# When the router's weights and the second norm's weight row are loaded, and when the output mixing waits for them

## The chip, the cores and the metric

The kernel runs on one core of one Trainium2 chip. The metric is the device time in microseconds (us) of one execution. The time of the kernel before is the median of three runs.

## The reference, cut to what matters

One layer of a hybrid model on 640 tokens (128 context, 512 latent), width D = 1024. The lines below follow the two scans; the change concerns `norm2_g` and the four `router_*` arrays.

```python
out = jnp.concatenate([o_r, o_g], -1) @ lp['w_out']          # o_r: RWKV-7 group, o_g: gated delta group
x = x + g1 * mix
h = rms_norm(x, lp['norm2_g']) * (1.0 + sc2) + sh2
grp_p = softmax(h @ router_group_w + router_group_b)          # 4 groups, top 1
e_logits = h @ router_expert_w + router_expert_b              # 32 experts, top 2 within the group
x = x + g2 * hier_moe(h, lp)                                  # gated MLP of the chosen experts
```

Inside the RWKV-7 group, before the concatenation, the scan's sum over both directions is normalised per head (lnx_g, lnx_b), a bonus term is added, and the result is multiplied by a gate, `sigmoid(gl) @ rwkv_g2`. The gated delta group is normalised (gdn_norm_g) and multiplied by silu(z).

## The kernel before, in words

The program is one list of instructions for each engine, ordered by hand; engines meet through semaphores. The stages are: the adaLN rows and the input projection, the gated delta scan, the RWKV scan (20 iterations, software pipelined in "slots"), the tail (output mixing, second norm, router, one token tile of 128 after another, five tiles), the sorting of tokens by expert, the experts in blocks, and the final norm. The change is at the seam between the RWKV scan and the tail.

SyncE (SP) issues nearly all loads, in program order. During the scan it stores `new_rwkv` from the tile `hTf` (columns 1536 to 2559, used as `znat`) and waits for the store (`rstate_out`, L473). It then waits for the last preparation step of the scan (L475 and L476) and issues the four constants of the mixing: `g2w`, `lnx_g`, `lnx_b`, `gng` (L477 to L480). Then it waits for the scan's last instruction (L481 and L482) and issues, in this order: `w_out` into `ring` (L483), `x` again (L484 context, L485 latent tokens), the two router weights (L486, L487), the two router biases (L488, L489), and `norm2_g` spread over all partitions into `bias_row` (L490). The last of these, and the five before it that are not `w_out` or `x`, count on the semaphore `cst_in`, nine loads in all.

TensorE (PE), after its last slot, waits for all nine (`pe.wait_ge(cst_in, 16 * 9)`, L973) and then does `mix_pe(0)`: four transposes of the scan's output (L983, "yT") and, when VectorE has subtracted the mean ("yc"), the gate's matmul (L986). It waits for `wout_in` (L1014) and goes through the tiles with `tail_pe(t)`: transposes of the mixed row tile (L993), `mix_pe(t + 1)`, the 16 products with `w_out` (L1001, 32 matmul records of the trace), transposes of the normed tile (L1006), and the router's products (L1010).

VectorE (DVE) waits for the nine constants and for `x` (L1934, L1935), makes the second norm's gain `modk[:, c, 2, :] = (1 + modk) * bias_row` for both conditionings (L1938, two instructions), and starts `mix_dve(0)`: from the reduction at L1957 to the product at L1981 ("o"), the whole of the mixing on one tile. `tail_dve(t)` does `mix_dve(t + 1)` first, then the residual (L1996, L1998), the norm (L2005, L2006) and the router's arithmetic (L2009 and on). Only `tail_dve` reads `x`, `modk[:, c, 2, :]` and the router's values; `mix_dve` reads none of them.

ScalarE (ACT) follows with squares, roots and copies out of PSUM (L1526 to L1549). It waits for none of these loads itself.

Of the kernel before, what the change touches and what calls it, by code (L numbers as in the profile page):

```python
# [10 lines left out]
ALU = mybir.AluOpType  # L11
# [3 lines left out]
P = 128  # L15
# [23 lines left out]
NE, GROUPS, PER_GROUP = 32, 4, 8  # L39
# [86 lines left out]
def program(nc, A, O, book, dbg=None):  # L126
    ctx = ExitStack()
    with ctx:
        sb = lambda name, shape, dt=F32: ctx.enter_context(nc.sbuf_tensor(name, shape, dt))
        sem = lambda name: ctx.enter_context(nc.semaphore(name))  # L130
# [4 lines left out]
        modk = sb("modk", [P, 2, 4, D])  # L135
# [6 lines left out]
        bias_row = sb("bias_row", [P, D])  # L142
# [20 lines left out]
        hTf = hT[:, :, :].rearrange("p k n -> p (k n)")  # L163
# [12 lines left out]
        work = fm[:, FM_V2:FM_V2 + 4, :].rearrange("p a b -> p (a b)")  # L176
# [30 lines left out]
        cst = fm[:, FM_Q2:FM_Q2 + 4, :].rearrange("p a b -> p (a b)")  # L207
        g2w, lnx_g, lnx_b, gng = cst[:, 0:512], cst[:, 512:1024], cst[:, 1024:1536], cst[:, 1536:1664]
        t_st, t_sgl, rtb = cst[:, 1664:1728], cst[:, 1728:1856], cst[:, 1856:1892]
        rw_ = work[:, 0:288].rearrange("p (k n) -> p k n", n=GROUPS + NE)  # L210
# [36 lines left out]
        ident_in, x_again = sem("ident_in"), sem("x_again")  # L247
# [13 lines left out]
        s_mix, s_tail, s_route, s_fin = ST("mix", True), ST("tail", True), ST("route", False), ST("fin", False)  # L261
        s_moe = ST("moe", True)
        wout_in, cst_in, h2_out, tz_out, tok_out, tok_in = (sem(n) for n in ("wout_in", "cst_in", "h2_out", "tz_out", "tok_out", "tok_in"))
# [141 lines left out]
        def _(sp):  # L405
# [67 lines left out]
            sp.wait_ge(rstate_out, 16)  # L473

# [7 lines left out]
            sp.wait_ge(*s_rwkv.pe.at(f"yz{R_ITS - 1}"))  # L482
            sp.dma_start(wout, A["w_out"][0].rearrange("(k p) n -> p k n", p=P)).then_inc(wout_in, 16)  # L483
            sp.dma_start(x[:, 0, :], A["x_prompt"][0]).then_inc(x_again, 16)  # L484
            sp.dma_start(x[:, 1:, :], A["x_sample"][0].rearrange("(t p) d -> p t d", p=P)).then_inc(x_again, 16)  # L485
            sp.dma_start(rw_[:, :, 0:GROUPS], A["router_group_w"][0].rearrange("(k p) n -> p k n", p=P)).then_inc(cst_in, 16)  # L486
            sp.dma_start(rw_[:, :, GROUPS:], A["router_expert_w"][0].rearrange("(k p) n -> p k n", p=P)).then_inc(cst_in, 16)  # L487
            sp.dma_start(rtb[:, 0:GROUPS], A["router_group_b"][0].partition_broadcast(P)).then_inc(cst_in, 16)  # L488
            sp.dma_start(rtb[:, GROUPS:], A["router_expert_b"][0].partition_broadcast(P)).then_inc(cst_in, 16)  # L489
            sp.dma_start(bias_row[:, :], A["norm2_g"][0].partition_broadcast(P)).then_inc(cst_in, 16)  # L490
# [39 lines left out]
        def _(pe):  # L530
# [442 lines left out]
            pe.wait_ge(cst_in, 16 * 9)  # L973
# [40 lines left out]
            pe.wait_ge(wout_in, 16)  # L1014
            tail_pe(0, True)
# [567 lines left out]
        def _(dve):  # L1583
# [350 lines left out]
            dve.wait_ge(cst_in, 16 * 9)  # L1934
            dve.wait_ge(x_again, 32)  # L1935
            dve.wait_ge(*s_route.act.at("silz"))
            for c in range(2):
                nc.vector.scalar_tensor_tensor(modk[:, c, 2, :], modk[:, c, 2, :], 1.0, bias_row[:, :], ALU.add, ALU.mult).then_inc(*s_route.dve.tick("gain2"))  # L1938
            dve.wait_ge(*s_route.dve.so_far())
# [100 lines left out]
            mix_dve(0)  # L2040
            tail_dve(0, 0)
# [56 lines left out]
            for t in range(NT):  # L2098
                c = min(t, 1)
# [36 lines left out]
```

## Time and profile before

| quantity | us |
|---|---|
| median of 3 runs | 2186.66 |
| lowest and highest of them | 2185.87, 2190.09 |
| profiled execution, its own time | 2192.51 |
| its span in the trace | 2190.6 |
| PE busy | 1660.5 (76% of the span) |
| DVE busy | 767.6 (35%) |
| ACT busy | 542.9 (25%) |

The span is what the trace covers; the execution's own time lies 1.91 us above it. Busy time over the span does not say what bounds a given stage. The page also cuts the span into 40 equal slices of 54.8 us and gives the busy share of each in tenths: in the 22nd, 1150 to 1205 us, which holds the end of the scan, it shows 4 tenths for PE, 2 for DVE and 3 for the DMA engines, and in the slice behind it 5, 6 and 0. The finer rows are in the section of rows below.

### The profile page before, as it was taken

To read this page: it belongs to the slowest core of one execution; us is meant where nothing else is said; L and a number is where in the kernel's file an instruction comes from. 1 tells how busy PE (TensorE), PEld (TensorE's weight loads), DVE (VectorE), ACT (ScalarE), POOL (GpSimd) and SP (SyncE) were. 2 spreads that over 40 slices of the span, in tenths; PEclk is the share of its full clock that TensorE was granted. 3 is DMA by queue.
4 is the path that set the end of the run, shared out by engine and by line. 5 is a ranking of instruction groups with operands and counts; after the bars stand their busy time and mean duration, and the time that the engine had idled before them with its cause. 6 is when DMAs were issued, how large, how long until landed. Compare 5 with 4: busy or idle time off the path is not lost. (4 is left out here: it accounts for less than half of the span.)

```text
span 2190.6 us, 36197 instructions
## 1 busy us (share of the span) xinstructions
PE 1660.5 (76%) x13628; PEld 1141.7 (52%) x13628; DVE 767.6 (35%) x1790; ACT 542.9 (25%) x1306; POOL 252.4 (12%) x481
## 2 busy tenths in 40 slices
PE   4999999889999858889994576527777777777740
PEld 3555664778888747777773334314444434334420
DVE  2000421445555546767772655301111111111114
ACT  2000236422323345555551112101000000000110
POOL 1000000311212142323220000010000000000001
PEclk9999989999999979999997687659889899888875
DMA  9343053000000000000003000089999999999952
GB/s 351 116 151 118 21 198 129 1 20 0 0 0 0 21 2 3 2 7 3 2 18 139 10 10 20 10 233 384 380 385 385 385 384 385 384 382 385 384 208 96
DMA packets 168736, 334.58 MB, mean 153 GB/s; under 512 B 24570, under 2 KB 41338, under 8 KB 168509
## 3 DMA queue, kind: packets, MB, share of 16 engines
q1 hardware_dynamic: 154656, 308.58, 39.0%
q0 software_dynamic: 4720, 14.95, 2.3%
q10 hardware_dynamic: 9264, 9.72, 1.4%
q8 instruction: 68, 1.11, 0.2%
q14 instruction: 28, 0.22, 0.0%
HBM read 303.85 MB, written 29.38 MB: 152 GB/s over the span
## 5 line engine op out<-in xcount | busy, mean ns | idle before, releaser
L1051 PE MATMUL ps<-ring,vz 128*64 128x256 f32 x1216 | 165.7, 440 | 52.7 <-DMA ring<-in_expert_up 50.3
L590 PE MATMUL ps<-hT,ring 128*128 128x320 f32 x704 | 197.8, 441 | 8.3 <-ACT hT L1253 5.5
L1051 PE MATMUL ps<-fm,vz 128*64 128x256 f32 x1152 | 157.1, 441 | 53.0 <-DMA fm<-in_expert_up 51.9
L590 PEld LDWEIGHTS ps<-hT,ring 128*128 128x128 f32 x704 | 135.7, 194 | 76.9 <-issue 19.5
L1051 PEld LDWEIGHTS ps<-ring,vz 128*64 128x64 f32 x1216 | 101.2, 160 | 111.2 <-issue 70.1
L1569 ACT ACT_TABLE_LOAD x37 | 47.5, 1283 | 433.6 <-DVE vz L2082 382.9
L2085 DVE TENSOR_TENSOR vz<-vz,ps 128x256 f32<-128x256 f32 x37 | 15.6, 421 | 394.0 <-PE ps L1051 394.0
L1051 PEld LDWEIGHTS ps<-fm,vz 128*64 128x64 f32 x1152 | 95.8, 160 | 108.7 <-issue 74.5
L1388 ACT COPY ring<-ps 64x256 f32<-64x256 f32 x200 | 73.3, 366 | 121.5 <-PE ps L793 119.0
L333 PE MATMUL ps<-ring 128*128 128x128 f32 x480 | 80.2, 290 | 9.2 <-DVE ring L378 8.8
L643 PE MATMUL ps<-ring,hT 128*128 128x512 f32 (+1 forms) x240 | 85.7, 512 | 0.8 <-PE ps L590 0.5
L1001 PE MATMUL ps<-ring,fm 128*128 128x512 f32 x160 | 78.7, 655 | 3.3 <-DVE fm L2035 3.3
L1062 PE MATMUL ps<-hT,vz 128*64 128x512 f32 x304 | 69.4, 598 | 13.4 <-DVE vz L2088 13.4
L802 PE MATMUL ps<-ring 128*64 128x64 f32 x1600 | 70.6, 233 | 10.2 <-ACT ring L1388 10.2
L2093 DVE COPY vz<-ps 128x512 f32<-128x512 f32 x37 | 25.6, 691 | 149.3 <-PE ps L1062 149.3
L793 PE MATMUL ps<-ring 128*64 128x64 f32 x1600 | 69.7, 231 | 8.7 <-DVE ring L1812 4.1
L356 ACT COPY ring<-ps 128x256 f32<-128x256 f32 x120 | 44.7, 372 | 124.7 <-PE ps L333 123.9
L1062 PE MATMUL ps<-fm,vz 128*64 128x512 f32 x288 | 65.8, 598 | 12.7 <-DVE vz L2088 12.7
L1812 DVE COPY_PREDICATED ring<-scr,ps 128x256 f32<-128x256 int32 x100 | 44.5, 445 | 87.8 <-PE ps L802 87.8
L344 PE MATMUL ps<-ring 128*128 128x128 f32 x480 | 74.2, 277 | 0.2
L333 PEld LDWEIGHTS ps<-ring 128*128 128x128 f32 x480 | 62.5, 190 | 20.7 <-DVE ring L378 18.4
L375 DVE COPY_PREDICATED ring<-tab,ps 128x256 f32<-128x256 int32 x100 | 44.4, 444 | 77.9 <-PE ps L340 77.7
(379 smaller groups left out, 2817.6 us busy)
## 6 DMA issues: line engine op xcount, KB each, us to landing
ring<-in_expert_gate SPq DMA_DIRECT2D x19, 2048.0 KB, 19.9
ring<-in_expert_up SPq DMA_DIRECT2D x19, 2048.0 KB, 24.0
hT<-in_expert_down SPq DMA_DIRECT2D x19, 2048.0 KB, 21.6
fm<-in_expert_gate SPq DMA_DIRECT2D x18, 2048.0 KB, 20.2
fm<-in_expert_up SPq DMA_DIRECT2D x18, 2048.0 KB, 23.9
fm<-in_expert_down SPq DMA_DIRECT2D x18, 2048.0 KB, 21.5
x<-in_ada_w SPq DMA_DIRECT2D x8, 2048.0 KB, 11.0
ring<-in_w_in SPq DMA_DIRECT2D x7, 2048.0 KB, 9.1
```

Of the source, the lines that this page charges most:

```text
L333: m = nc.tensor.matmul(ps[d][:, P * hh:P * (hh + 1)], lt(s_), i_x[:, s_, :], start=True, stop=True)
L344: m = nc.tensor.matmul(ps[4 + d][:, P * hh:P * (hh + 1)], i_y[:, s_, :], i_xt[:, s_, :], start=True, stop=True)
L356: nc.scalar.copy(pair(i_y, d), ps[d][:, 0:256].rearrange("p (s n) -> p s n", n=P)).then_inc(*S.tick(f"y{k}{d}"))
L590: m = nc.tensor.matmul(ps[2 * (job % 2) + g][:, 0:HALF], ring[:, u, k, P * ct:P * (ct + 1)], hT[:, k, HALF * g:HALF * (g + 1)], start=k == ...
L643: m = nc.tensor.matmul(ps[4 + q % 4][:, 0:nc_], hT[:, k, P * t:P * (t + 1)], ring[:, u, k, 0:nc_], start=k == 0, stop=k == KD - 1)
L793: i = nc.tensor.matmul(ps[0][RD * h:RD * (h + 1), RD * s_:RD * (s_ + 1)], r_sc[par][:, s_, RD * h:RD * (h + 1)], r_x[par][:, s_, :], start ...
L802: i = nc.tensor.matmul(ps[1][RD * h:RD * (h + 1), RD * s_:RD * (s_ + 1)], r_xt[par][:, s_, :], r_y[:, s_, RD * h:RD * (h + 1)], start=True ...
L1001: m = nc.tensor.matmul(ps[3 + b][:, :], oT[:, k, :], wout[:, k, 512 * b:512 * (b + 1)], start=k == 0, stop=k == KD - 1)
L1051: m = nc.tensor.matmul(ps[bank][BT * h:BT * (h + 1), 0:256], e_xT[u][:, k, :], w_[:, k, 256 * h:256 * (h + 1)], start=k == 0, stop=k == KD ...
L1062: m = nc.tensor.matmul(ps[5][BT * h:BT * (h + 1), :], e_hT[u][:, n % 2, n // 2, :], wd[:, n, 512 * h:512 * (h + 1)], start=n == 0, stop=n ...
L1388: then(nc.scalar.copy(r_y[rows, :, rows], ps[0][rows, 0:256].rearrange("p (s n) -> p s n", n=RD)), f"y{k}_{it}")
L1569: nc.scalar.activation(e_h[u], ps[2][:, 0:256], ACT.Silu).then_inc(*S.tick(f"silu{u}"))
```

## The change

The router's two weights and two biases get another home, columns 1536 to 1859 of `hTf`, which is free once `new_rwkv` is stored; they are issued there, right after the wait for that store, and count on a semaphore of their own, `router_in`. `norm2_g` counts on its own semaphore too, `norm2_in`, and is issued first at the scan's end, ahead of `w_out` and `x`. What waited for nine loads waits for the four that are left on `cst_in`; VectorE's waits for `norm2_g` and `x`, and the gain, come after `mix_dve(0)`; the waits for the router's values come ahead of `tail_pe(0)` and `tail_dve(0)`.

```diff
-        t_st, t_sgl, rtb = cst[:, 1664:1728], cst[:, 1728:1856], cst[:, 1856:1892]
-        rw_ = work[:, 0:288].rearrange("p (k n) -> p k n", n=GROUPS + NE)
+        t_st, t_sgl = cst[:, 1664:1728], cst[:, 1728:1856]
+        rw_, rtb = hTf[:, 1536:1824].rearrange("p (k n) -> p k n", n=GROUPS + NE), hTf[:, 1824:1860]
...
+        norm2_in, router_in = sem("norm2_in"), sem("router_in")
...
             sp.wait_ge(rstate_out, 16)
+            sp.dma_start(rw_[:, :, 0:GROUPS], A["router_group_w"][0].rearrange("(k p) n -> p k n", p=P)).then_inc(router_in, 16)
+            sp.dma_start(rw_[:, :, GROUPS:], A["router_expert_w"][0].rearrange("(k p) n -> p k n", p=P)).then_inc(router_in, 16)
+            sp.dma_start(rtb[:, 0:GROUPS], A["router_group_b"][0].partition_broadcast(P)).then_inc(router_in, 16)
+            sp.dma_start(rtb[:, GROUPS:], A["router_expert_b"][0].partition_broadcast(P)).then_inc(router_in, 16)
...
             sp.wait_ge(*s_rwkv.pe.at(f"yz{R_ITS - 1}"))
+            sp.dma_start(bias_row[:, :], A["norm2_g"][0].partition_broadcast(P)).then_inc(norm2_in, 16)
             sp.dma_start(wout, A["w_out"][0].rearrange("(k p) n -> p k n", p=P)).then_inc(wout_in, 16)
             sp.dma_start(x[:, 0, :], A["x_prompt"][0]).then_inc(x_again, 16)
             sp.dma_start(x[:, 1:, :], A["x_sample"][0].rearrange("(t p) d -> p t d", p=P)).then_inc(x_again, 16)
-            sp.dma_start(rw_[:, :, 0:GROUPS], A["router_group_w"][0].rearrange("(k p) n -> p k n", p=P)).then_inc(cst_in, 16)
-            sp.dma_start(rw_[:, :, GROUPS:], A["router_expert_w"][0].rearrange("(k p) n -> p k n", p=P)).then_inc(cst_in, 16)
-            sp.dma_start(rtb[:, 0:GROUPS], A["router_group_b"][0].partition_broadcast(P)).then_inc(cst_in, 16)
-            sp.dma_start(rtb[:, GROUPS:], A["router_expert_b"][0].partition_broadcast(P)).then_inc(cst_in, 16)
-            sp.dma_start(bias_row[:, :], A["norm2_g"][0].partition_broadcast(P)).then_inc(cst_in, 16)
...
-            pe.wait_ge(cst_in, 16 * 9)
+            pe.wait_ge(cst_in, 16 * 4)
...
             mix_pe(0)
             pe.wait_ge(wout_in, 16)
+            pe.wait_ge(router_in, 16 * 4)
             tail_pe(0, True)
...
-            dve.wait_ge(cst_in, 16 * 9)
-            dve.wait_ge(x_again, 32)
+            dve.wait_ge(cst_in, 16 * 4)
             dve.wait_ge(*s_route.act.at("silz"))
-            for c in range(2):
-                nc.vector.scalar_tensor_tensor(modk[:, c, 2, :], modk[:, c, 2, :], 1.0, bias_row[:, :], ALU.add, ALU.mult).then_inc(*s_route.dve.tick("gain2"))
-            dve.wait_ge(*s_route.dve.so_far())
...
             mix_dve(0)
+            dve.wait_ge(norm2_in, 16)
+            dve.wait_ge(x_again, 32)
+            for c in range(2):
+                nc.vector.scalar_tensor_tensor(modk[:, c, 2, :], modk[:, c, 2, :], 1.0, bias_row[:, :], ALU.add, ALU.mult).then_inc(*s_route.dve.tick("gain2"))
+            dve.wait_ge(*s_route.dve.so_far())
+            dve.wait_ge(router_in, 16 * 4)
             tail_dve(0, 0)
```

## Rows read from the trace of the kernel before

**Rows 1.** Waits from 1178 to 1245 us: engine, line, releaser: us in total, times, longest.
```profile
DVE modk L1938 <- DMA bias_row<-in_norm_g: 23.8, 1, 23.8
```

**Rows 2.** Timeline at the scan's end: start us, us, engine, line, operation, out<-in.
```profile
1177.77 0.43 PE L898 MATMUL ps<-fm,scr 128*64 128x64 f32 x4
1178.64 0.28 DVE L1887 TENSOR_TENSOR hT<-ps,hst 128x128 f32<-128x128 f32 x1
```

**Rows 3.** Timeline of SP's queue behind the scan's end.
```profile
1178.96 0.38 SPq L483 DMA_DIRECT2D ring<-in_w_out  x1
1180.00 0.43 SPq L485 DMA_DIRECT2D x<-in_x_sample  x1
1180.48 4.43 SPq L486 DMA_DIRECT2D fm<-in_router_group_w  x1
...
1198.52 0.43 SPq L490 DMA_DIRECT2D bias_row<-in_norm_g  x1
```

**Rows 4.** DMA issues, 1178 to 1215 us: transfer, KB, us from issue to landing.
```profile
ring<-in_w_out SPq DMA_DIRECT2D x1, 4096.0 KB, 12.8
x<-in_x_sample SPq DMA_DIRECT2D x1, 2048.0 KB, 18.6
bias_row<-in_norm_g SPq DMA_DIRECT2D x1, 512.0 KB, 4.2
fm<-in_router_group_w SPq DMA_DIRECT2D x1, 16.0 KB, 18.5
```

**Rows 5.** Windows: stretch, its us, busy us by engine, PEclk, DMA share, GB/s.
```profile
1186.00:1190.00 4.00, 0.00 (x0) 0.00 (x0) 0.00 (x0) 0.00 (x0) 0.00 (x0) 0.50 1.02 417
...
1197.00:1198.00 1.00, 0.00 (x0) 0.00 (x0) 0.00 (x0) 0.00 (x0) 0.00 (x0) 0.50 1.23 200
...
1201.00:1202.00 1.00, 0.00 (x0) 0.00 (x0) 0.00 (x0) 0.00 (x0) 0.00 (x0) 0.50 0.85 307
```

**Rows 6.** Timeline from the norm's landing to the first residual.
```profile
1202.75 2.36 DVE L1938 SCALAR_TENSOR_TENSOR modk<-modk,bias_row 128x1024 f32<-128x1024 f32 x2 [23.83 <-DMA bias_row<-in_norm_g]
1205.26 0.69 DVE L1957 TENSOR_REDUCE fm<-ps 128x8 f32<-128x512 f32 x1
1217.63 1.94 PE L993 MATMUL ps<-tab,fm 128*128 128x128 f32 x8 [8.62 <-DVE fm L1981]
1220.53 0.69 DVE L1957 TENSOR_REDUCE fm<-ps 128x8 f32<-128x512 f32 x1 [3.04 <-PE ps L983]
...
1239.18 0.69 DVE L1996 TENSOR_TENSOR fm<-ps,modk 128x512 f32<-128x512 f32 x1 [4.82 <-PE ps L1001]
```

**Rows 7.** Chain of work: products with w_out, tiles 0, 1 and 4: start us, us.
```profile
1224.28 14.81 PE ps L1001 x32
...
1260.74 15.35 PE ps L1001 x32
...
1368.17 16.41 PE ps L1001 x32
```

**Rows 8.** Windows at the start of tiles 0 and 4, columns as in rows 5.
```profile
1220.00:1224.00 4.00, 2.22 (x4) 0.85 (x4) 2.57 (x6) 0.82 (x2) 0.00 (x0) 0.50 0.00 0
...
1368.00:1372.00 4.00, 3.83 (x5) 1.79 (x6) 0.44 (x3) 0.03 (x1) 0.00 (x0) 0.50 0.00 0
```

**Rows 9.** The page's groups: a VectorE operation in the experts, under their loads.
```profile
L2093 DVE COPY vz<-ps 128x512 f32<-128x512 f32 x37 | 25.6, 691 | 149.3 <-PE ps L1062 149.3
```

**Rows 10.** SP's queue in the scan: its wait, then timeline rows.
```profile
SPq L476 <- DVE fm L1804: 152.8, 1, 152.8
974.00 0.64 SPq L472 DMA_DIRECT2D out_new_rwkv<-hT  x1
1129.55 0.43 SPq L480 DMA_DIRECT2D fm<-in_gdn_norm_g  x1
```

**Rows 11.** DMA issue of the state's store, columns as in rows 4.
```profile
out_new_rwkv<-hT SPq DMA_DIRECT2D x1, 256.0 KB, 3.5
```

**Rows 12.** The page's DMA queues: kind: packets, MB, share of 16 engines.
```profile
q8 instruction: 68, 1.11, 0.2%
```

## The prediction

> **What bounds the kernel now.** I read in this order: the page's slices (PE, DVE and the DMA engines all fall in the slice with the scan's end), then the waits of that stretch, the timeline of SP's queue, the landings, and last the timeline behind them, to see which wait really sets the date of the first long matmul group.
>
> The waits say that DVE stood still for 23.8 us until `norm2_g` landed [rows 1]; PE's wait at L973 is for the same semaphore. The scan's last PE group ends at 1177.77 + 0.43 = 1178.2 us and its last DVE instruction at 1178.64 + 0.28 = 1178.92 us [rows 2]. SP then issues `w_out` at 1178.96, the latent `x` at 1180.00, and the norm row at 1198.52, because the four router loads keep SP's queue from 1180.48 to 1198.52, 18.04 us [rows 3]. With the landings: `w_out` is there at 1178.96 + 12.8 = 1191.8, `x` at 1180.00 + 18.6 = 1198.6, the group weights at 1180.48 + 18.5 = 1199.0, the norm row at 1198.52 + 4.2 = 1202.7 [rows 3, 4]. The gain starts at 1202.75 [rows 6], so the norm row ends the wait. But this is only the first link. Behind it lie, one after another: the gain (until the reduction at 1205.26, 2.51 us after 1202.75), `mix_dve(0)` (1205.26 to the transposes at 1217.63, 12.37 us), PE's transposes (1217.63 to 1220.53, 2.90 us), and then `mix_dve(1)`, whose third instruction releases the gate's matmul, behind which the products with `w_out` stand in PE's order [rows 6]. So the number to move is the 1220.53 at which `mix_dve(1)` starts.
>
> **The change part by part.**
>
> Narrower wait ahead of `mix(0)`. The last of the four loads left on `cst_in` was issued at 1129.55 [rows 10], 49 us before the scan ends; the broadcast of 512 KB took 4.2 us to land [rows 4]. So the wait is met, PE can transpose from 1178.2 and DVE starts at about 1179.0, as soon as its last scan instruction is done. `mix_dve(0)` takes the same 12.37 us and ends at about 1191.4. It runs while the stream lands. The nearest row for a DVE operation under a stream is the 128x512 copy in the experts, 691 ns [rows 9], and the 128x512 and reduction steps here show 0.69 us without one [rows 6]; I charge nothing for the overlap. The cover is wide: `x` lands at about 1200, 8.5 us after 1191.4, so `mix_dve(0)` would have to take 1.7 times as long before it cost anything.
>
> `norm2_g` first. It delays `w_out` and `x`. Its bytes, 512 KB or 0.524 MB, at the stream's 417 GB/s [rows 5] are 1.3 us. The lower bound is nothing, if it only fills the start of the stream; the upper one is its whole 4.2 us from issue to landing [rows 4]. I take 1.3, since the stream is full from the start and its price there is its share. When it ran alone the rate was only 307 GB/s [rows 5], by which it is 1.7. `w_out` then lands at about 1193.1, `x` at 1198.6 + 1.3 = 1199.9.
>
> Router loads away from this place. Their packets stand behind `x`; group weights landed 0.4 us after `x` [rows 3, 4]. From 1197 to 1198 the DMA engines are fully busy at 200 GB/s instead of 417 [rows 5], which is small packets mixed with the end of `x`. So taking them away may give `x` something, at most the half of that microsecond, 0.5 us, and at least nothing. I take nothing and keep 0.5 in the range. The Trainium skill ("DMA: Bandwidth & Descriptors", section "Queues, rings and completion order") has each DMA engine take descriptors in ring order, by which packets queued behind `x` cannot delay it on its own engine; the sum by it is the one taken, and by the mixed second of the rows it would be 0.5 us lower. That the group weights landed after `x` agrees with the page.
>
> Router loads at the new place. SP stored the state at 974.00 and it landed 3.5 us later [rows 10, 11]; the four issues follow at 977.5. SP then had 152.8 us of waiting before L477 [rows 10], against 18.04 us of issuing in the worst case [rows 3], so nothing behind them in its queue moves, and no scan instruction reads what they load. Cost zero with that cover; without it, up to 18.04 us of issue and the last landing. On the side of a gain there is nothing, since no instruction of the scan leaves. The two waits on `router_in` are met 200 us early. The two `slot_token` stores, issued behind L490, now go out some 18 us earlier, and their reader sits behind the whole tail; zero.
>
> The gain after `mix_dve(0)`. DVE waits at `x` until 1199.9; queued behind that wait are the gain and all of `mix_dve(1)`, and PE's gate matmul and products wait for that. The gain and its wait are 2.51 us, so `mix_dve(1)` starts at 1202.4. PE is ready: it passes `wout_in` at 1193.1 and needs 2.90 us for the transposes, 1196.0, which is 6.4 us early. The norm row, issued first, is there long before.
>
> Sum: 1220.53 − 1202.4 = 18.1 us earlier. What is late next is `x`, with 20.9 us between the scan's end and its landing.
>
> Behind that date the order of work is as it was: `mix_dve(1)` is hidden under the products, since its 12.4 us end before the second half of them. One term is left, TensorE's clock. The granted clock is 0.50 (1.2 GHz) at the start of tile 0 and of tile 4 alike [rows 8], and the products take 14.81, 15.35 and 16.41 us in tiles 0, 1 and 4, five tiles in all, tile 0 being the shortest [rows 7]. In the changed kernel PE stands idle from 1196.0 until `yc` of tile 1, at about 1204.1, 8 us instead of 1.78, so I expect it no better than tile 1: 15.35 − 14.81 = 0.5 us lost, with 0 and 16.41 − 14.81 = 1.6 as ends. Net: 18.1 − 0.5 = 17.6 us.
>
> The expert stage begins that much earlier and does the same.
>
> The profiled execution took 2192.51 us, 1.91 above its span of 2190.6, so the changed one by this sum is 2174.9 with a span of 2173.0. The median of the runs shown is 2186.66, 5.85 below the profiled one; against it the sum gives 2186.66 − 17.6 = 2169.1 us.
>
> **The rivals.**
>
> Whole stream dearer or cheaper. If the norm row costs nothing and `x` gains the 0.5, `x` lands at 1198.1 and, with no clock loss, the gain is 1220.53 − 2.51 − 1198.1 = 19.9 us: 2166.7. If the norm row holds the stream up by all of its 4.2 us, `x` lands at 1202.8 and the gain, with 1.6 of clock, is 13.6 us: 2173.1. For it speaks that every packet of a broadcast reads the same row, which alone ran at 307 instead of 417 GB/s [rows 5].
>
> Clock. In tile 0 all products run at 1.2 GHz because PE has idled longer. The 14.81 us contain some cold matmuls already; all cold is at most twice 14.81, so it costs at most 14.8 us, and the gain shrinks to 18.1 − 14.8 = 3.3 us: 2183.4. Against it: tile 4 starts at 0.50 as well and still needs only 16.41 [rows 7, 8]. The Trainium skill ("TensorE: Matmul & The Clock Gate", section "HAM oscillation — how this bites in real kernels") says that a wait between bursts makes each following burst start cold; this change makes such a wait longer. The clock rows agree that each tile starts cold, and show that it does so before the change too.
>
> The wait goes elsewhere and the early start fails. If `mix(0)` still waited for something that comes with the stream, only the norm row's lateness would go: 1202.7 − 1199.9 = 2.8 us, 2183.9. The four issue dates [rows 10] speak against it.
>
> Slower. The moved router loads starve the scan: instructions are fetched through DMA queues of the core too [rows 12], and if these fetches were held behind the small packets, the scan would stand still while these are issued and land, at 977.5 us, by up to 18.04 + 4.2 = 22.2 us [rows 3, 4]. It decides from 17.6 us of stall on; at its full price the kernel is 22.2 − 17.6 = 4.6 us slower, 2191.3. Against it: the state's store, 256 KB in small pieces at the same place, landed in 3.5 us [rows 11], and behind the scan the issue was slow with a full stream ahead of it, which is not there at 977.5.
>
> **How the numbers follow.** Chances: the forecast 0.76, the dearer or cheaper stream 0.13, the clock 0.04, the early start that fails 0.03, the starved scan 0.04. A run of this kernel spreads from 2185.87 to 2190.09, so I widen the forecast's own interval (terms: 0.9 less or 2.9 more for the stream, 0.5 less or 1.1 more for the clock) by some 2 us: 2164.5 to 2174.0, which also holds both ends of the stream. 0.2% is 4.4 us, about what a measurement can tell from no change. Faster holds the forecast, the stream's case, half of the clock's (its price is a most) and a quarter of the starved scan's: 0.76 + 0.13 + 0.02 + 0.01 = 0.92. Slower holds half of the starved scan's, 0.02. The rest, 0.06, is no change.
>
> **What would show it.** In the changed trace `mix_dve(0)`'s first reduction should start within a microsecond of the scan's last DVE instruction, and its transposes' group on PE at about the landing of `w_out`; DVE's next long wait should end with `x`, not with `norm2_g`, 20 to 21.5 us after the scan's end; the second reduction at L1957 should start 23.5 us after the scan's last DVE instruction instead of 41.6; the scan's end should keep its date within a microsecond; the products of tile 0 should take 15 to 16.4 us. The prediction is wrong if the scan ends later, if `x` lands over 24 us after its end, or if the time from L1957 of tile 1 to the end of the tail grows.

## The result, and the profile after

The changed kernel takes 2173.98 us (median of 6 runs, 2169.88 to 2177.0) where the kernel before takes 2188.53 (6 runs, 2185.87 to 2192.0): ratio 0.9931, 95% interval 0.9915 to 0.9947. Timed a second time it took 2173.48 us against 2191.21, ratio 0.9919, interval 0.9904 to 0.9934. The forecast was 2169.1 with a range of 2164.5 to 2174.0 and a gain of 17.6 us; the two timings give 14.6 and 17.7.

In the profiled executions the span falls from 2190.6 to 2171.4 us, 19.2 us. Part of that is not the change's. The scan's steps show it: DVE's last instruction of the scan ends at 1178.92 us before [rows 2] and at 1177.26 after, 1.66 us earlier, and the shift is already there at 970 us, before the first instruction that was changed (rows of the end of two scan steps, first before, then after; between them lie the four router loads in the changed kernel only).

```profile
971.44 0.28 DVE L1887 TENSOR_TENSOR hT<-ps,hst 128x128 f32<-128x128 f32 x1
993.23 0.28 DVE L1887 TENSOR_TENSOR hT<-ps,hst 128x128 f32<-128x128 f32 x1
```

```profile
969.78 0.28 DVE L1889 TENSOR_TENSOR hT<-ps,hst 128x128 f32<-128x128 f32 x1
991.57 0.28 DVE L1889 TENSOR_TENSOR hT<-ps,hst 128x128 f32<-128x128 f32 x1
```

Both pairs are 21.79 us apart. So from here on I read every trace on a clock of its own that starts at the end of the scan's last DVE instruction. It takes the spread of what lies before out of the comparison: over the traces below the scan ended between 1174.3 and 1182.4 us.

Selected lines of the timeline after, from the scan's end to the first residual (these answer to rows 2, 3 and 6):

```profile
1176.46 0.81 PE L984 MATMUL ps<-tab,fm 128*128 128x128 f32 x4
1176.98 0.28 DVE L1889 TENSOR_TENSOR hT<-ps,hst 128x128 f32<-128x128 f32 x1
1177.30 0.33 SPq L488 DMA_DIRECT2D bias_row<-in_norm_g  x1
1177.32 0.69 DVE L1955 TENSOR_REDUCE fm<-ps 128x8 f32<-128x512 f32 x1
1177.68 0.42 SPq L489 DMA_DIRECT2D ring<-in_w_out  x1
...
1178.76 0.64 SPq L491 DMA_DIRECT2D x<-in_x_sample  x1
...
1188.86 0.69 DVE L1979 TENSOR_TENSOR fm<-fm,vz 128x512 f32<-128x512 f32 x1
1192.28 1.97 PE L994 MATMUL ps<-tab,fm 128*128 128x128 f32 x8 [12.16 <-DMA ring<-in_w_out]
1194.04 1.06 PE L984 MATMUL ps<-tab,fm 128*128 128x128 f32 x4
1198.72 2.36 DVE L2042 SCALAR_TENSOR_TENSOR modk<-modk,bias_row 128x1024 f32<-128x1024 f32 x2 [9.16 <-DMA x<-in_x_sample]
1201.11 0.69 DVE L1955 TENSOR_REDUCE fm<-ps 128x8 f32<-128x512 f32 x1
1202.79 2.07 PE L987 MATMUL ps<-fm 128*128 128x512 f32 x2 [7.69 <-DVE fm L1957]
1204.66 15.34 PE L1002 MATMUL ps<-ring,fm 128*128 128x512 f32 x32
1220.11 0.69 DVE L1994 TENSOR_TENSOR fm<-ps,modk 128x512 f32<-128x512 f32 x1 [5.16 <-PE ps L1002]
```

Read it in this order. `mix_dve(0)` starts 0.06 us after the scan and is over at 1189.55, under the stream; all its 128x512 steps still take 0.69 us. PE's transposes wait for `w_out`, DVE's gain waits for `x`, and the second reduction at L1955, where `mix_dve(1)` starts, comes 23.85 us after the scan where it came at 41.61. The landings (columns as in rows 4):

```profile
ring<-in_w_out SPq DMA_DIRECT2D x1, 4096.0 KB, 14.6
x<-in_x_sample SPq DMA_DIRECT2D x1, 2048.0 KB, 19.8
bias_row<-in_norm_g SPq DMA_DIRECT2D x1, 512.0 KB, 4.5
```

| us from the scan's end to | before | after | difference |
|---|---|---|---|
| w_out landed | 12.84 | 15.02 | +2.2 |
| x landed | 19.68 | 21.30 | +1.6 |
| start of mix(1) | 41.61 | 23.85 | −17.76 |
| residual's second half, tile 0 | 60.26 | 42.85 | −17.41 |
| first expert load issued | 244.13 | 227.03 | −17.10 |
| end of the span | 1011.68 | 994.14 | −17.54 |

### The profile page after: what moved, and what is told of

Same layout as the page of the kernel before. It is cut to its first block, busy times and chain, and to the rows that moved or that the text cites. A ratio compares the mean times of both kernels' runs of the same rounds, so it can differ in the third digit from the quotient of the medians.

```text
span 2171.4 us, 36197 instructions
## 1 busy us (share of the span) xinstructions
PE 1662.4 (77%) x13628; PEld 1143.1 (53%) x13628; DVE 767.5 (35%) x1790; ACT 542.9 (25%) x1306; POOL 252.4 (12%) x481
## 4 chain that ended last, share of the span: by engine, by line
PE 22%; DMA 14%; SPq 12%; DVE 8%; issue 3%; ACT 2%; POOL 1%; POOLq 0%; DVEq 0%; ACTq 0%
DMA fm<-in_expert_up 8%; SPq L516 6%; PE ps L1053 5%; SPq L518 4%; PE ps L1002 4%; DMA ring<-in_expert_up 3%; PE ps L794 2%; PE ps L803 2%; SPq L515 2%; PE ps L762 2%; PE ps L846 1%; DMA fm<-expert_rows,gi 1%; DMA x<-in_x_sample 1%; DVE ring L1814 1%; PE ps L1011 1%
## 5 line engine op out<-in xcount | busy, mean ns | idle before, releaser
L591 PEld LDWEIGHTS ps<-hT,ring 128*128 128x128 f32 x704 | 135.4, 194 | 76.6 <-issue 19.2
## 6 DMA issues: line engine op xcount, KB each, us to landing
fm<-in_expert_down SPq DMA_DIRECT2D x18, 2048.0 KB, 21.8
```

Source lines behind the costliest of these rows:

```text
L591: m = nc.tensor.matmul(ps[2 * (job % 2) + g][:, 0:HALF], ring[:, u, k, P * ct:P * (ct + 1)], hT[:, k, HALF * g:HALF * (g + 1)], start=k == ...
```

## The experiments

Each table row below is read from one trace of that kernel on the clock from the scan's end, all in us; "second residual" is the residual's second half of tile 0. The first lines are the kernel before and the changed one, which was traced twice.

| kernel | w_out | x | mix(1) | second residual | first expert load | median us | ratio to before (95%) |
|---|---|---|---|---|---|---|---|
| before | 12.8 | 19.7 | 41.61 | 60.26 | 244.13 | 2188.53 | 1 |
| changed | 15.0 | 21.3 | 23.85 | 42.85 | 227.03 | 2173.98 | 0.9931 (0.9915 to 0.9947) |
| changed, second time | 14.9 | 21.2 | 23.75 | 42.03 | 225.55 | 2173.48 | 0.9919 (0.9904 to 0.9934) |
| e1 wide waits | 14.9 | 21.3 | 39.23 | 57.36 | 240.79 | 2188.79 | 0.9988 (0.9975 to 1.0001) |
| e2 router loads behind x | 15.0 | 21.8 | 24.31 | 42.88 | 226.67 | 2172.02 | 0.9916 (0.9899 to 0.9934) |
| e3 norm row last | 13.3 | 19.7 | 23.43 | 42.86 | 227.50 | 2175.72 | 0.9923 (0.9907 to 0.9940) |
| e4 gain after mix(1) | 14.9 | 21.3 | 17.88 | 36.30 | 220.00 | 2169.33 | 0.9894 (0.9877 to 0.9912) |
| e5 and w_out first | 13.1 | 19.5 | 16.07 | 32.71 | 216.48 | 2162.68 | 0.9876 (0.9859 to 0.9894) |
| e6 changed, PE kept busy | 14.9 | 21.2 | 23.75 | 40.40 | 222.27 | 2170.37 | 0.9921 (0.9901 to 0.9940) |
| e7 router loads three times | 14.8 | 21.2 | 23.70 | 42.77 | 227.04 | 2173.64, one run | |
| e8 e5, products ahead of the gate | 13.2 | 19.6 | 16.18 | 32.44 | 206.77 | 2153.42 | 0.9833 (0.9818 to 0.9848) |
| e9 e8, PE kept busy | 13.6 | 20.1 | 16.62 | 33.03 | 191.36 | 2138.62 | 0.9758 (0.9741 to 0.9774) |

The ratios of e1 to e4, of e5 to e8, and of e9 with the second timing of the changed kernel are each against their own runs of the kernel before (medians 2191.92, 2190.18 and 2191.21).

The two traces of the changed kernel say how far such a row can be relied on. They start mix(1) within 0.1 us of each other, but the second residual lies 0.8 us apart and the first expert load 1.5. Nearly all of that is TensorE's clock: the products of tile 0 took 15.34 us in the first and 14.63 in the second. The granted clock (columns as in rows 5, PEclk is the third number from the end) shows the rise from 0.50 to 1.00. Here is the stretch that holds it, in the first trace, whose products start at 1204.66, and in the second, whose products start at 1201.87:

```profile
1206.00:1208.00 2.00, 2.00 (x4) 0.84 (x3) 1.58 (x4) 0.21 (x1) 0.00 (x0) 0.61 0.00 0
```

```profile
1202.00:1204.00 2.00, 2.00 (x5) 0.84 (x4) 1.55 (x5) 0.21 (x1) 0.00 (x0) 0.66 0.00 0
```

A mean of 0.61 puts the rise at 1207.56, 2.9 us into the products, and one of 0.66 puts it at 1203.36, 1.5 us into them. So behind mix(1) a difference of 1 us or so can be the clock's alone.

**e1: the loads moved, the waits wide.**

```diff
 pe.wait_ge(cst_in, 16 * 4)
+pe.wait_ge(norm2_in, 16)
+pe.wait_ge(x_again, 32)
...
 dve.wait_ge(*s_route.act.at("silz"))
+dve.wait_ge(norm2_in, 16)
+dve.wait_ge(x_again, 32)
+for c in range(2):
+    nc.vector.scalar_tensor_tensor(modk[:, c, 2, :], ...)
+dve.wait_ge(*s_route.dve.so_far())
+dve.wait_ge(router_in, 16 * 4)
...
 mix_dve(0)
-dve.wait_ge(norm2_in, 16)
-dve.wait_ge(x_again, 32)
-for c in range(2):
-    nc.vector.scalar_tensor_tensor(modk[:, c, 2, :], ...)
-dve.wait_ge(*s_route.dve.so_far())
-dve.wait_ge(router_in, 16 * 4)
 tail_dve(0, 0)
```

> The loads stand as in the changed kernel, but PE and DVE again wait for norm2_g and x (and DVE makes the gain) ahead of mix(0). Read on a clock that starts at the end of the scan's last DVE instruction; mix(1) starts at 41.6 us in the kernel before and 23.9 in the changed one. Theory A (the gain comes from starting mix(0) under the stream; the landing of x plus the gain sets mix(1)): x lands at 21.4, then 2.5 for the gain, 12.4 for mix(0), 2.9 for the transposes: mix(1) at 39.2, the kernel 2.4 us faster than before. Theory B (the gain comes from the loads that were moved out of SP's queue): mix(1) stays near 24, the kernel 15 to 18 us faster than before.

Measured: mix(1) at 39.23 us, 2.38 earlier than before, and a median 3.1 us below that of its runs of before, though the interval of its ratio, 0.9975 to 1.0001, just reaches no change. Theory A to a tenth; B, with mix(1) near 24, is out. DVE's one long wait, by the waits of its trace (columns as in rows 1), now ends with `x`:

```profile
DVE modk L1943 <- DMA x<-in_x_sample: 21.4, 1, 21.4
```

So the loads' new places alone are worth 2.4 us, and the narrower waits 39.23 − 23.85 = 15.4. The other order, narrow waits with the loads left in their old places, was not run; from rows 4 and 6 (the norm row there 23.8 us after the scan, then 2.5 for the gain) I estimate mix(1) at 26.3 us, which would split the 17.8 in the same way.

**e2: the router loads back behind x.**

```diff
 sp.wait_ge(rstate_out, 16)
-sp.dma_start(rw_[:, :, 0:GROUPS], A["router_group_w"]...).then_inc(router_in, 16)
-sp.dma_start(rw_[:, :, GROUPS:], A["router_expert_w"]...).then_inc(router_in, 16)
-sp.dma_start(rtb[:, 0:GROUPS], A["router_group_b"]...).then_inc(router_in, 16)
-sp.dma_start(rtb[:, GROUPS:], A["router_expert_b"]...).then_inc(router_in, 16)
...
 sp.dma_start(x[:, 1:, :], A["x_sample"]...).then_inc(x_again, 16)
+sp.dma_start(rw_[:, :, 0:GROUPS], A["router_group_w"]...).then_inc(router_in, 16)
+sp.dma_start(rw_[:, :, GROUPS:], A["router_expert_w"]...).then_inc(router_in, 16)
+sp.dma_start(rtb[:, 0:GROUPS], A["router_group_b"]...).then_inc(router_in, 16)
+sp.dma_start(rtb[:, GROUPS:], A["router_expert_b"]...).then_inc(router_in, 16)
...
 pe.wait_ge(wout_in, 16)
-pe.wait_ge(router_in, 16 * 4)
...
 pe.wait_ge(*s_tail.act.at("h2T1", it))
+pe.wait_ge(router_in, 16 * 4)
...
 dve.wait_ge(*s_tail.pe.at("logits", it))
+dve.wait_ge(router_in, 16 * 4)
```

> The changed kernel with the four router loads back behind x at the scan's end (into the new home), waited for only where the router's values are first used, 45 us later. Theory A (moving the router loads out is worth nothing by itself once the waits are narrow): mix(1) at 23.9 us after the scan, the time as the changed kernel within 0.5 us. Theory B (their packets mix with the end of x, or SP's 18 us of issuing hold something up): x lands 0.5 us or more later, mix(1) at 24.4 or later.

Measured: `x` lands 0.5 us later and mix(1) starts at 24.31, 0.46 later than in the changed kernel's first trace and 0.56 later than in its second. Here B's number came, and A's was wrong in that step: with the small packets behind it `x` lands later (21.8 us, against 21.2 to 21.3 in all six traces with the norm row first and no router loads there). At the second residual the first trace no longer shows it (42.88 against 42.85), because the products took 14.92 and not 15.34 us; that is the spread of the clock, and the second trace has 42.03. The median, 2172.02, is that of the changed kernel within the intervals. SP's issuing of the four took 19.4 us (18.0 before), as the rows of its queue show, and nothing waited for it:

```profile
1176.58 5.63 SPq L488 DMA_DIRECT2D hT<-in_router_group_w  x1
1182.27 9.75 SPq L489 DMA_DIRECT2D hT<-in_router_expert_w  x1
1192.06 3.43 SPq L490 DMA_DIRECT2D hT<-in_router_group_b  x1
```

**e3: the norm row last.**

```diff
-sp.dma_start(bias_row[:, :], A["norm2_g"]...).then_inc(norm2_in, 16)
 sp.dma_start(wout, A["w_out"]...).then_inc(wout_in, 16)
 sp.dma_start(x[:, 0, :], A["x_prompt"][0]).then_inc(x_again, 16)
 sp.dma_start(x[:, 1:, :], A["x_sample"]...).then_inc(x_again, 16)
+sp.dma_start(bias_row[:, :], A["norm2_g"]...).then_inc(norm2_in, 16)
```

> The changed kernel with norm2_g issued behind x and not first. Theory A (the row takes its share of the stream, 1.3 us): w_out lands at 13.7 us after the scan and not 15.0, x at 20.1 and not 21.4, and the row itself 1.3 to 2 us after x, so mix(1) starts where it did, 23.9 to 24.5. Theory B (the row is free at the head of the stream): w_out and x land as in the changed kernel, the row 1.3 to 2 us after x, and mix(1) starts at 25.2 to 26.

Measured: `w_out` 1.7 us and `x` 1.6 us earlier, the norm row at 20.95, 1.3 us behind `x`, mix(1) at 23.43. Theory A in its mechanism; its size was too small: the row takes more than 1.3 us at the head. Over all traces, `w_out` lands 12.8 to 13.6 us after the scan where it leads the stream (five traces, mean 13.2) and 14.8 to 15.0 where the row does (seven, mean 14.9). The windows show where (columns as in rows 5). In the changed kernel the stream's start runs below its later rate while the DMA engines are already busy at 93% and 99%:

```profile
1180.00:1182.00 2.00, 0.12 (x1) 0.00 (x0) 1.90 (x4) 0.90 (x1) 0.00 (x0) 0.56 0.93 324
1182.00:1184.00 2.00, 0.00 (x0) 0.00 (x0) 1.54 (x5) 0.21 (x1) 0.00 (x0) 0.50 0.99 356
1184.00:1186.00 2.00, 0.00 (x0) 0.00 (x0) 1.86 (x5) 0.00 (x0) 0.00 (x0) 0.50 1.02 422
```

In these stretches of 2 us it comes to 422 GB/s from 6.7 us behind the first issue on. In e3, whose first issue is at 1179.74, it is there 4.3 us behind it:

```profile
1182.00:1184.00 2.00, 0.42 (x1) 0.00 (x0) 1.88 (x4) 1.21 (x1) 0.00 (x0) 0.79 0.96 371
1184.00:1186.00 2.00, 0.00 (x0) 0.00 (x0) 1.54 (x5) 0.21 (x1) 0.00 (x0) 0.50 1.05 422
```

Which end of the stream the row takes moves mix(1) by 0.3 to 0.4 us (23.43 against 23.85 and 23.75), since the row and `x` are waited for together. The second residual (42.86) and the median show nothing of it: the products took 15.78 us here, the longest of all traces.

**e4: the gain behind mix(1).**

```diff
     mix_dve(it + 1)
+if not c:
+    dve.wait_ge(norm2_in, 16)
+    dve.wait_ge(x_again, 32)
+    for q in range(2):
+        nc.vector.scalar_tensor_tensor(modk[:, q, 2, :], ...)
+    dve.wait_ge(*s_route.dve.so_far())
+    dve.wait_ge(router_in, 16 * 4)
...
 mix_dve(0)
-dve.wait_ge(norm2_in, 16)
-dve.wait_ge(x_again, 32)
-for c in range(2):
-    nc.vector.scalar_tensor_tensor(modk[:, c, 2, :], ...)
-dve.wait_ge(*s_route.dve.so_far())
-dve.wait_ge(router_in, 16 * 4)
 tail_dve(0, 0)
```

> The changed kernel with DVE's waits for norm2_g and x, and the gain, moved behind mix_dve(1), ahead of the first residual. Theory A (x and the gain are what mix(1) waits for): mix(1) starts when PE's transposes are done, w_out at 15.0 plus 2.9, so at 18.0 us after the scan and not 23.9; mix(1) ends at 30.3, the gain at 32.8, the products at about 37, so all 5.8 us are kept and the kernel is 5.8 us faster than the changed one. Rival B (DVE becomes late: 2.4 us of gain more stand ahead of the first residual): the residual's second half does not start with the products' end but up to 2.4 us behind it, and 3.4 us are kept.

Measured: mix(1) at 17.88, 5.9 to 6.0 us earlier; the second residual at 36.30, 6.55 us earlier than in the first trace of the changed kernel and 5.7 than in the second, and DVE still waits there for PE:

```profile
1199.60 0.69 DVE L1955 TENSOR_REDUCE fm<-ps 128x8 f32<-128x512 f32 x1 [5.71 <-PE ps L984]
1211.88 2.36 DVE L1989 SCALAR_TENSOR_TENSOR modk<-modk,bias_row 128x1024 f32<-128x1024 f32 x2
1218.02 0.69 DVE L2001 TENSOR_TENSOR fm<-ps,modk 128x512 f32<-128x512 f32 x1 [2.19 <-PE ps L1002]
```

Theory A. In the changed kernel it is `x` and the gain that mix(1) waits for, and neither is needed there. Median 2169.33 against 2173.5 to 2174.0; this difference, 4.2 to 4.7 us, is smaller than the traces' 5.6 to 7.0 us, and the intervals of the ratios (0.9877 to 0.9912, and 0.9904 to 0.9934 for the changed kernel) overlap. The earlier dates are shown, the gain in time is not clear of the spread.

**e5: w_out first as well.** e4 with e3's order of loads.

> The kernel e4 with norm2_g issued behind x, so w_out leads the stream. Theory A (behind the late gain, w_out's landing and PE's transposes set mix(1)): w_out lands at 13.3 us after the scan as in e3, mix(1) starts at 16.2 and not 17.9; the residual's second half stands 1.7 us earlier than in e4 (34.6 after the scan), and the kernel is 8 us faster than the changed one. Rival B: mix(0) itself, 12.3 us from the scan's end, or the norm row's later landing (21 us after the scan, needed at 28.5) gets in the way: 17.9 or later.

Measured: `w_out` at 13.1, mix(1) at 16.07, 1.8 us earlier than in e4, as A had it. The second residual moved by 3.6, more than that, because the clock was up by then: the gate's matmuls took 1.13 us and the products 13.90, against 2.07 and 14.76 in e4. That half of the 3.6 I don't put down to the edit: PE's pause ahead of the gate is the same in e4 (1.79 us) as here (1.78), and why the clock rose earlier was not isolated. The median, 2162.68, is 11 us below the changed kernel's where A had 8.

```profile
1193.01 1.13 PE L987 MATMUL ps<-fm 128*128 128x512 f32 x2 [1.78 <-DVE fm L1957]
1193.97 13.90 PE L1002 MATMUL ps<-ring,fm 128*128 128x512 f32 x32
```

**e6: the clock.** `keep_clock(bank, n)` is in the kernel before already: n products of the identity with itself.

```diff
 m.then_inc(*s_mix.pe.tick("yT"))
+if it == 1:
+    keep_clock(7, 24)
```

> The changed kernel with 24 dummy products of the identity on PE, into a PSUM bank that nothing else uses then, behind the transposes of tile 1, where PE would stand idle for 7.7 us. Theory A (what the products of tile 0 lose to TensorE's clock is at most what cold matmuls cost): the gate's matmul group takes 1.1 us and not 2.07 and the products 13.8 to 14.0 and not 15.3, so the residual's second half stands 2.3 to 2.5 us earlier. Rival B (PE at 2.4 GHz doesn't help since DVE releases it): no change beyond 0.5 us; or the dummies run into the gate's matmul and cost up to 2 us.

Measured: gate 1.12 us, products 13.90, second residual 2.45 us earlier than in the changed kernel's first trace: A. Against its second trace it is 1.63 us. The gate took 2.07 or 2.08 us in all five other traces with this long wait, so the effect is there, and its size is 1.6 to 2.5 us. The granted clock of the stretch ahead of the gate is 1.00 (2.4 GHz) in e6 and 0.50 (1.2 GHz) in the changed kernel:

```profile
1193.00:1199.00 6.00, 4.88 (x44) 4.69 (x42) 3.22 (x4) 0.00 (x0) 0.00 (x0) 1.00 0.28 107
1199.00:1203.00 4.00, 3.24 (x8) 1.57 (x9) 3.08 (x6) 0.63 (x1) 0.00 (x0) 1.00 0.02 4
```

```profile
1196.00:1202.00 6.00, 0.00 (x0) 0.00 (x0) 3.21 (x4) 0.00 (x0) 0.00 (x0) 0.50 0.28 108
1202.00:1206.00 4.00, 3.21 (x4) 1.50 (x5) 3.06 (x7) 0.63 (x1) 0.00 (x0) 0.50 0.00 0
```

I had not expected what followed: tiles 1 to 4, unchanged in the program, were shorter too, 14.48, 15.29, 15.69 and 16.26 us where the changed kernel has 15.71, 15.90, 16.00 and 16.42. These are 2.3 us more, so the first expert load came 4.76 us earlier. Against the second trace (15.36, 15.72, 15.91 and 16.36 us) they are 1.6 us, and the load 3.3. The sooner behind their start the clock rises, the shorter are a tile's products (tile 0 above: 1.5 us and 14.63, 2.9 us and 15.34). That the earlier dates of tile 0 made the later tiles shorter here is argued and not shown: in e5 tile 0 took 13.90 us too, and tile 1 15.46. What sets the date of the rise was not isolated. The median, 2170.37, is 3 us below the changed kernel's, which the intervals do not tell apart.

**e7: the router loads three times in the scan.**

```diff
 sp.dma_start(rw_[:, :, 0:GROUPS], A["router_group_w"]...).then_inc(router_in, 16)
 sp.dma_start(rw_[:, :, GROUPS:], A["router_expert_w"]...).then_inc(router_in, 16)
 sp.dma_start(rtb[:, 0:GROUPS], A["router_group_b"]...).then_inc(router_in, 16)
 sp.dma_start(rtb[:, GROUPS:], A["router_expert_b"]...).then_inc(router_in, 16)
+sp.wait_ge(router_in, 16 * 4)
+sp.dma_start(rw_[:, :, 0:GROUPS], A["router_group_w"]...).then_inc(router_in, 16)
+sp.dma_start(rw_[:, :, GROUPS:], A["router_expert_w"]...).then_inc(router_in, 16)
+sp.dma_start(rtb[:, 0:GROUPS], A["router_group_b"]...).then_inc(router_in, 16)
+sp.dma_start(rtb[:, GROUPS:], A["router_expert_b"]...).then_inc(router_in, 16)
+sp.wait_ge(router_in, 16 * 8)
+sp.dma_start(rw_[:, :, 0:GROUPS], A["router_group_w"]...).then_inc(router_in, 16)
+sp.dma_start(rw_[:, :, GROUPS:], A["router_expert_w"]...).then_inc(router_in, 16)
+sp.dma_start(rtb[:, 0:GROUPS], A["router_group_b"]...).then_inc(router_in, 16)
+sp.dma_start(rtb[:, GROUPS:], A["router_expert_b"]...).then_inc(router_in, 16)
```

> The changed kernel with the four router loads issued three times in the scan, each set after the one before has landed. Theory A (in the scan they are free): the scan ends within the spread that kernels with one set or none show (1174 to 1182 us), its steps around 980 us take as long as before, mix(1) 23.9 us after the scan. Rival B (they slow the scan, each set by s): the stretch of the scan from 974 to 1010 us is 2s longer, where s would have to be over 1 us to matter.

Measured: the two scan steps around them are 21.79 us apart, as in the kernel before, and each load landed in 2.4 to 3.4 us:

```profile
970.31 0.28 DVE L1899 TENSOR_TENSOR hT<-ps,hst 128x128 f32<-128x128 f32 x1
992.10 0.28 DVE L1899 TENSOR_TENSOR hT<-ps,hst 128x128 f32<-128x128 f32 x1
```

The step behind them took 17.54, 17.54 and 17.55 us in the kernel before, the changed one and this one. Theory A; s is nothing that the trace can show.

**e8: the products ahead of the gate.** The experiments show PE idle for 4.6 us in every later tile, waiting for `yc` although the operands of the products are there; tile 1 of the changed kernel:

```profile
1239.60 2.08 PE L987 MATMUL ps<-fm 128*128 128x512 f32 x2 [4.62 <-DVE fm L1957]
```

e8 is e5 with

```diff
 m.then_inc(*s_mix.pe.tick("yT"))
+def gate_pe(it):
     pe.wait_ge(*s_mix.dve.at("yc", it))
     nc.tensor.matmul(ps[0][:, :], fm[:, FM_LORA + 1, P * it:P * (it + 1)], g2w, ...)
...
     for b in range(2):
...
         m.then_inc(*S.tick(f"mix{b}"))
+        if more and b == 0:
+            gate_pe(it + 1)
...
 mix_pe(0)
+gate_pe(0)
```

> The kernel e5 with PE's order in the tail changed: the gate's matmul of the next tile, which waits for DVE's yc, stands between the two halves of the products with w_out and no longer ahead of both. Theory A (in every tile PE waits 4.6 us for yc with all operands of the products there but the copies of oT, which ScalarE ends 0.5 us before DVE starts mix): the products start 3 to 4 us earlier in tiles 1 to 3, 1.5 in tile 0, so 10 to 13 us less than e5. Rival B: DVE's chain through mix becomes the bound, as it ends 12.3 us after it starts and the first residual waits for it: under 4 us less.

Measured: the first expert load 9.7 us earlier than in e5 and a median 9.3 us lower, just under A's 10 to 13 and far above B's 4. Tile 0 gave 0.3 and not 1.5, and there it is rival B that holds. Its products end 30.96 us after the scan where e5's end at 32.61, so PE did become 1.65 us earlier. But DVE has no pause left: mix(1), the gain and the residual's first half run into the second half, which starts at 32.44, 1.5 us behind the products:

```profile
1205.44 7.03 PE L1004 MATMUL ps<-ring,fm 128*128 128x512 f32 x16
1209.97 2.36 DVE L1994 SCALAR_TENSOR_TENSOR modk<-modk,bias_row 128x1024 f32<-128x1024 f32 x2
1213.95 0.69 DVE L2006 TENSOR_TENSOR fm<-ps,modk 128x512 f32<-128x512 f32 x1
```

In tile 1, which has no gain in it, DVE again waits for the products there, by 2.68 us. PE waits 2.5 us a tile now, and the clock takes part of it back: the first half of the products, at 1.2 GHz for its first part, takes 8.8 us and the second 7.0.

```profile
1231.28 8.80 PE L1004 MATMUL ps<-ring,fm 128*128 128x512 f32 x16 [2.54 <-DVE fm L2045]
1239.91 1.02 PE L989 MATMUL ps<-fm 128*128 128x512 f32 x2
1240.77 7.03 PE L1004 MATMUL ps<-ring,fm 128*128 128x512 f32 x16
```

**The changed kernel again, and e9.**

> The changed kernel itself once more, for a narrower interval. Its trace and that of the kernel before give 17.1 us between the scan's end and the first expert load, the six timed runs 14.6 between the medians (interval 12 to 19). Theory A (the seam's 17.1 us reach the end undiminished, and the difference is the spread of runs): a median 16 to 18 us under that of before. Rival B (some 2 to 3 us are given back in the expert stage): 13 to 15 us.

Measured: 17.7 us between the medians, mix(1) at 23.75, first expert load at 225.55. Theory A for the time. The two timings of the same pair of kernels, 14.6 and 17.7 us, show how far a difference of medians can be relied on here. The trace itself looks like rival B: the stage of the experts, from its first load to the end of the span, took 771.2 us in it, where it took 767.1 in the first trace and 767.5 before. Of all twelve traces ten have 767.0 to 768.3 us and only this one and e8's 771.2 and 771.0; nothing in the seam explains that, and its cause stays open. e9 is e8 with

```diff
+if it:
+    keep_clock(6, 12)
 pe.wait_ge(*s_tail.dve.at("x2", it, 1))
...
+keep_clock(6, 24)
 pe.wait_ge(*s_tail.dve.at("h2", it))
```

> The kernel e8 with dummy products of the identity on PE in its two idle stretches of a tile, into the bank of the h2 transposes that nothing uses then: 24 behind the products (idle 6.4 us for the norm), 12 behind the transposes of the next tile (idle 2.5 us for DVE and ScalarE). Theory A (the tail runs mostly at 1.2 GHz because PE idles between bursts, and the clock is worth in every tile what e6 showed in tile 0): the first half of the products takes 6.9 us and not 8.8, the h2 transposes 1.0 and not 2.0, the router's products 2 and not 3.6, so 4 us or more per tile: 15 to 20 us less than e8. Rival B (the dummies keep PE from the real work, or the clock still falls): gain under 5 us or a loss.

Measured: the first expert load 15.4 us earlier than in e8, the median 14.8 us lower, the one just inside A and the other just under it. Tile 0 has no part in it: the first half of its products took 8.77 us and not 7.25 as in e8, though the program is the same up to there, and its second residual came 0.6 us later. The timeline of tile 0's end and tile 1's start, with the dummies as L316:

```profile
1215.17 5.52 PE L316 MATMUL ps<-tab 128*128 128x128 f32 x48
1221.43 1.10 PE L1014 MATMUL ps<-tab,fm 128*128 128x128 f32 x8 [0.74 <-DVE fm L2019]
1223.26 1.98 PE L1018 MATMUL ps<-hT,fm 128*128 128x36 f32 x16 [0.73 <-ACT fm L1554]
...
1230.29 7.11 PE L1006 MATMUL ps<-ring,fm 128*128 128x512 f32 x16 [1.04 <-DVE fm L2048]
...
1253.40 3.63 PE L1018 MATMUL ps<-hT,fm 128*128 128x36 f32 x16 [0.73 <-ACT fm L1554]
1256.83 1.95 PE L996 MATMUL ps<-tab,fm 128*128 128x128 f32 x8
```

In the same place PE's work takes about half as long when the clock is held (1.10 for 1.97 us and 1.98 for 3.63); in tile 1 it still fell once, at about 1253 to 1260 us, and the router's products took 3.63 us again. e9 is the fastest version, 2138.62 us, ratio 0.9758 to the kernel before.

## Why the prediction held, point by point

The mechanism is the one that was forecast, and e1 shows it. Two of its small terms were off, one is open, and that the time lies inside the range owes something to luck.

The early start of mix(0) and the link that is late next: right. The prediction put `mix_dve(0)` at 1179.0, that is 0.1 us after the scan, its length at 12.37 us, 12.22 to the end of "o" (12.23 measured, from 1177.32 to 1189.55), and `x` as what ends the next wait. e1 shows the size: 15.4 of the 17.8 us are the waits' width. (The nine loads of the wide wait are the four constants, the four router loads and the norm row.)

The norm row at the head of the stream: right mechanism, too small. I priced it at the stream's own rate, 1.3 us. The means over the traces give 1.7 for `w_out`. I had a row that gives this number (307 GB/s when alone, hence 1.7) and took the other; that the two agree does not show that they have one cause.

The router loads behind `x`: I took nothing for their removal, with 0.5 as the other end. e2 shows 0.5 to 0.6 in the landing of `x`, so the term should have been 0.5. Between before and after `x` lands 1.6 later, and that is both terms together: about 2.1 for the row less 0.5 for the packets, where I had 1.3 less nothing. How the 2.1 and the 1.7 go together was not separated; in e3 the row itself stands behind `x` and may hold it up as the packets do. The Trainium skill ("DMA: Bandwidth & Descriptors", section "Queues, rings and completion order") has descriptors consumed in ring order on each engine, by which I had chosen the nothing. That was my step and not the page's: the same sentence of it lets a later descriptor finish its write before an earlier one, so it does not promise that what stands behind `x` leaves it alone. e2 measures half a microsecond, and the measurement decides.

The sum at mix(1): 18.1 forecast, 17.76 and 17.86 measured in the two traces; the 0.3 is `x`, which landed 1.6 us later and not 1.3.

The clock: 0.5 us lost was forecast for the products of tile 0, because PE would stand idle for 8 us instead of 1.78. The pause came (7.69 us); the loss is not shown. Against 15.00 us before (by the timelines) the first trace has 15.34, a loss of 0.34, and the second, of the same kernel, 14.63, a gain of 0.37. Over all traces in which PE does this work in the same order, the short pause has 15.00, 14.47, 14.76 and 13.90 us (before, e1, e4, e5) and the long one 15.34, 14.63, 14.92, 15.78 and 15.42 (changed twice, e2, e3, e7). The mean of the long ones is 0.7 higher, the way that was forecast, but the ranges overlap. So the size of this term is open, and the sign given for it, 15 to 16.4 us, held in the first trace and not in the second. The forecast had nothing for the later tiles, and they move the same way: together they add 0.3 us in the first trace and take 0.4 off in the second. Hence 17.1 and 18.6 us at the first expert load, on either side of 17.8. The Trainium skill ("TensorE: Matmul & The Clock Gate", section "HAM oscillation — how this bites in real kernels") has the burst behind a long enough wait start cold. The gate's 2.07 us behind the long pause agree, but it took 2.07 us behind the 1.78 us of the kernel before as well, since the clock was at 0.50 there too [rows 8]; e6 and e9 show what filling the pauses is worth, 1.6 to 2.5 us in one tile and 14.8 us over the tail.

The net gain: 17.6 forecast; 17.1 at the first expert load and 17.5 at the span's end in the first trace, 18.6 and 14.9 in the second, whose expert stage was the long one; 14.6 and 17.7 between medians.

The absolute time: 2173.98 and 2173.48 measured, 2169.1 forecast, with a range that ends at 2174.0. That the first lies inside, by 0.02 us, is luck where runs of one kernel spread by 6 us. The range was not added up well either: the lower end of the stream's terms is 1.3 + 0.5 = 1.8 us less and not 0.9, and with 2.9 and 1.1 more and some 2 for the spread its upper end would be about 2175.1. In the second timing the whole of the 4.4 us is the base: the gain is 17.7, but the kernel before ran at 2191.2, not at 2186.66, the median of the first three runs (all sets of it since: 2188.5 to 2191.9). In the first, 1.9 of the 4.9 us are the base and 3.0 the smaller difference. The profiled execution as a base, 2192.51 − 17.6 = 2174.9, comes nearer, but it is a single one too.

Two signs of error need a word. The scan's end was to keep its date within a microsecond; it moved by 1.66 us and in the second trace by 4.3, ahead of the change, so the sign was narrower than the spread. And the time from L1957 of tile 1 to the end of the tail was not to grow; to the first expert load it grew by 0.7 us in the first trace and shrank by 0.7 in the second, which is the clock again.

The rivals. That the early start fails is out by e1 and the timeline. The starved scan is out: 21.79 us for the same steps with none, one and three sets of router loads. A whole tile at 1.2 GHz didn't happen: the clock is at 1.00 from 2.9 and 1.5 us into the products of tile 0. The dearer stream is what moved the sum, by 0.3 us and not by 4.

## What to carry to other kernels

When a wait counts many loads, list what the instructions behind it really read; here the first tile's mixing read four of nine, and 15.4 of 17.8 us came from the wait's width, not from the loads' new places. Then do it again one link further: the changed kernel still waited for `x` and a gain ahead of work that reads neither, worth about 6 us more by the traces (e4; between medians 4 to 5, with overlapping intervals). A forecast of an absolute time needs a base of more runs than three when runs spread by 6 us; the gain and the base should be given separately. And a term of half a microsecond for TensorE's clock can't be read from one trace: two traces of the same kernel differed by more.

## What the runs showed of the hardware that I had not expected

A row of 4 KB spread over 128 partitions (512 KB written) costs a full stream 1.6 us (`x`, e3 against the changed kernel) to 1.7 us (`w_out`, over the traces' means) at its head, where the stream's rate of 417 GB/s would make it 1.3. Issuing the two router weights takes 4.4 to 9.8 us each of SP's queue behind a full stream, and in the scan, where nothing stood ahead of them, 0.4 to 0.6 us. It is not their small pieces alone: in the changed kernel the `slot_token` store of 9.8 KB stands there and takes 4.76 us. The same kernel's products of tile 0 took 15.34 and 14.63 us in two executions, because the clock rose 2.9 and 1.5 us into them. A burst of dummy products in one tile's pause, e6, brought the second residual forward by 1.6 to 2.5 us; the four later tiles, which were not touched, were 1.23, 0.61, 0.31 and 0.16 us shorter than in the first of those executions and 0.88, 0.43, 0.22 and 0.10 than in the second. Holding the clock through the tail's pauses, e9, gave 14.8 us, nearly as much as the change that this document is about.
